# The recurrent layer's gates laid between its projections, a core eviction ahead of a scaling, and the MLP residual by token tile

## What is computed

```
# recurrent layer
u = hn @ w_in + b_in ; x_br = u[:, :1024] ; y_br = gelu(u[:, 1024:])
xc = conv_b + sum over 4 taps of x_br[t-3+tap] * conv_w[tap]
r  = sigmoid(xc_block @ w_ga + b_ga) ; ig = sigmoid(xc_block @ w_gx + b_gx)   # 8 blocks of 128
log_a = -8 * r * softplus(-a_param) ; a = exp(log_a)
b_seq = sqrt(-expm1(2*log_a)) * ig * xc
hs[t] = a[t]*hs[t-1] + b_seq[t]
h = h + (hs * y_br) @ w_o + b_o
# MLP
z = relu(rmsnorm(h) @ w1) ; h = h + (z*z) @ w2
# RWKV-7, after the state scan
y = (y - mean) * rsqrt(var + eps) * lnx_g + lnx_b + bonus * v ; out = (y * silu(g)) @ w_out
```

## Time and profile before

| | us |
|---|---|
| median of 3 runs (lowest to highest) | 1199.31 (1197.18 to 1202.8) |
| the profiled execution | 1200.37 |
| its span | 1198.6 |
| TensorE busy | 1075.3 (90%) |
| GpSimd, ACT, VectorE busy | 706.1, 535.0, 486.0 |
| stretch of the recurrent layer | 332 to 442 |
| second MLP | 443.8 to 623.7 |
| RWKV core and its state steps | 755 to 878 |

### The profile page before, as it was taken

The page is one execution under the profiler, slowest core; times in us unless marked ns, Lnnn a source line. Parts: engine busy times, 40 slices in busy tenths (PEclk is TensorE's granted clock), DMA queues, the critical chain, the costliest instruction groups (busy, mean ns, idle before and its releaser), DMA issues. The chain is left out here.

```text
span 1198.6 us, 19877 instructions
## 1 busy us (share of the span) xinstructions
PE 1075.3 (90%) x8416; PEld 883.7 (74%) x8416; DVE 486.0 (41%) x654; ACT 535.0 (45%) x834; POOL 706.1 (59%) x443
## 2 busy tenths in 40 slices
PE   5999999999977699999988999898898869989685
PEld 4788898998877689999964445798846557767554
DVE  1124274352366725321247266435641451223232
ACT  5537374444436755444421151222223564559352
POOL 6956459988837579989830025300035849667660
PEclk8999999999988899999998999899999979999798
DMA  9642345555634345555572343000036425423140
GB/s 367 235 141 71 133 152 190 191 184 189 193 115 151 123 155 180 192 184 187 191 228 88 114 149 123 20 4 3 4 123 223 159 89 192 133 96 123 62 157 36
DMA packets 45848, 169.37 MB, mean 141 GB/s; under 512 B 5088, under 2 KB 5344, under 8 KB 45440
## 3 DMA queue, kind: packets, MB, share of 16 engines
q1 hardware_dynamic: 43312, 159.06, 39.8%
q0 software_dynamic: 2448, 9.05, 2.4%
HBM read 167.03 MB, written 1.05 MB: 140 GB/s over the span
## 5 line engine op out<-in xcount | busy, mean ns | idle before, releaser
L692 POOL TENSOR_TENSOR ring_r<-ring,high_r 128x512 fp32r<-128x512 f32 (+1 forms) x368 | 635.0, 1755 | 263.5 <-ACT high_r L846 262.2
L846 ACT CAST high_r<-ring 128x1024 fp32r<-128x1024 f32 x248 | 256.5, 1048 | 245.8 <-DMA ring<-w 243.5
L424 PE MATMUL psum<-x_high,high_r 128*128 128x256 f32 x640 | 182.6, 285 | 1.6 <-DVE x_low L282 1.6
L424 PE MATMUL psum<-x_low,high_r 128*128 128x256 f32 x640 | 181.5, 284 | 0.0
L424 PE MATMUL psum<-x_high,ring_r 128*128 128x256 f32 x640 | 181.4, 283 | 0.0
L398 PE MATMUL psum<-high_r,x_high 128*128 128x512 f32 x320 | 131.4, 411 | 13.1 <-DVE x_low L278 9.4
L398 PE MATMUL psum<-ring_r,x_high 128*128 128x512 f32 x320 | 128.7, 402 | 0.0
L398 PE MATMUL psum<-high_r,x_low 128*128 128x512 f32 x320 | 128.7, 402 | 0.0
L600 DVE TENSOR_TENSOR arena<-arena 128x512 f32<-128x512 f32 x32 | 51.7, 1616 | 183.5 <-ACT arena L576 183.4
L424 PEld LDWEIGHTS psum<-x_high,high_r 128*128 128x128 f32 x640 | 123.2, 192 | 2.9 <-issue 1.3
L424 PEld LDWEIGHTS psum<-x_low,high_r 128*128 128x128 f32 x640 | 123.2, 192 | 0.6
(11 more groups left out here) (309 smaller groups left out, 1616.6 us busy)
## 6 DMA issues: line engine op xcount, KB each, us to landing
ring<-w SPq DMA_DIRECT2D x292, 512.0 KB, 3.4
row<-rows POOLq DMA_DIRECT2D x14, 512.0 KB, 8.4
arena<-relt SPq DMA_DIRECT2D x2, 1536.0 KB, 14.8
h<-x SPq DMA_DIRECT2D x1, 1024.0 KB, 5.1
arena<-lora POOLq DMA_DIRECT2D x2, 512.0 KB, 6.2
out<-h SPq DMA_DIRECT2D x1, 1024.0 KB, 4.0
con<-consts SPq DMA_DIRECT2D x1, 529.0 KB, 5.5
arena<-pT POOLq DMA_DIRECT2D x2, 256.0 KB, 4.0
```

The source lines that it names most:

```text
L424: ins = nc.tensor.matmul(out, a, b, start=(k == 0 and q == 0), stop=(k == KT - 1 and q == 2))
L692: ins = nc.gpsimd.tensor_tensor(low(m)[:, part], raw(m)[:, part], read(high(m))[:, part], ALU.subtract)
L846: nc.scalar.copy(high(m), raw(m)).then_inc(high_made, 1)
```

## The change

1. **Residual by tile.** The last row piece of each MLP raises `w2_tile0` when token tile 0 is complete; VectorE adds tile 0 behind that and tile 1 behind the last piece.
2. **Recurrent layer.** The pieces are laid out anew (`REC`, `REC_AT`): x0 to x5, g0, x6, x7, g1, y0, y1, g2, g3, y2 to y7, and TensorE works in that order. ACT evicts x twice (with its bias to `xb`; and with bias `cb` and scale conv_w3, which is the last tap, to `xc`), and VectorE makes the other three taps. The sigmoids become Tanh of half the argument; factors 4 and 0.25 and a "+1" take up the rest. The first half's decays come after gate group 1, the second's after group 3. The products with y, the high copies and the low parts go by quarters instead of halves; the six first casts of W_RO stand ahead of the high copies. GpSimd waits for `scan_done` 2 before W_RO's pieces 0 and 1, and for `og_low` 4 before all later ones. b_o is added after the last low part.
3. **RWKV.** `scale_shift` is cut in `rescale` and `weight_bias`. For the first half they move from ahead of group 1's last eviction to behind `first_state(1)` and behind `next_state(1, 1)`.

```diff
+REC = ["x0", "x1", "x2", "x3", "x4", "x5", "g0", "x6", "x7", "g1", "y0", "y1", "g2", "g3", "y2", "y3", "y4", "y5", "y6", "y7"]
+REC_AT = {name: 4 * W_REC + i for i, name in enumerate(REC)}
...
-            used_piece(dve, w2_piece(m, 7, 3))
             for t in range(NT):
+                if t == 0:
+                    dve.wait_ge(w2_tile0, m + 1)
+                else:
+                    used_piece(dve, w2_piece(m, 7, 3))
...
+                            if c == 7 and f == 3 and t == 0:
+                                ins.then_inc(w2_tile0, 1)
...
+            low_until(4 * W_RO)
+
+            pool.wait_ge(scan_done, 2)
+            low_until(4 * W_RO + 2)
+            pool.wait_ge(og_low, 4)
             low_until(4 * W_RKVG)
...
+            def conv_start(i):
+
+                used_piece(act, REC_AT[f"x{2 * i + 1}"])
                 for j in range(2):
                     f = 2 * i + j
+                    nc.scalar.activation(xb[:, f, 3:], psum[:, i, j * SEQ:(j + 1) * SEQ], ACT.Identity, bias=c8("b_in_x")[:, f:f + 1])
+                    ins = nc.scalar.activation(xc[:, f, :], psum[:, i, j * SEQ:(j + 1) * SEQ], ACT.Identity, bias=cb[:, f:f + 1],
+                                               scale=c8("conv_w3")[:, f:f + 1])
+                ins.then_inc(x_read, 1)
+                split_until(min(REC_AT[f"x{2 * i + 1}"] + 1 + RING, 4 * W_RO))
+
+            def gates_out(i):
+
+                used_piece(act, REC_AT[f"g{i}"])
+                for j in range(2):
+                    f = 2 * i + j
+                    nc.scalar.activation(rg[:, f, :], psum[:, 4 + i % 2, j * SEQ:(j + 1) * SEQ], ACT.Tanh,
+                                         bias=half_ga[:, f:f + 1], scale=0.5)
+                    ins = nc.scalar.activation(ig[:, f, :], psum[:, 6 + i % 2, j * SEQ:(j + 1) * SEQ], ACT.Tanh,
+                                               bias=half_gx[:, f:f + 1], scale=0.5)
                 ins.then_inc(gates_read, 1)
+                split_until(min(REC_AT[f"g{i}"] + 1 + RING, 4 * W_RO))
+
+            split_until(REC_AT["x0"] + RING)
+            conv_start(0)
+            conv_start(1)
+            conv_start(2)
+            act.wait_ge(decay_ready, 1)
+            gates_out(0)
+            conv_start(3)
+            gates_out(1)
...
+            act.wait_ge(gates_read, 2)
+            decays_of(0)
+            gates_out(2)
+            gates_out(3)
             act.wait_ge(gates_read, 4)
+            decays_of(1)
             for q in range(2):
                 act.wait_ge(m2_ready, q + 1)
+                nc.scalar.activation(th[:, 4 * q:4 * q + 4, :], th[:, 4 * q:4 * q + 4, :], ACT.Sqrt,
+                                     scale=0.25).then_inc(m_ready, 1)
             for i in range(4):
+                used_piece(act, REC_AT[f"y{2 * i + 1}"])
...
                 ins.then_inc(y_read, 1)
+                if i >= 1:
+                    split_until(4 * W_RO + 2 * i)
+            for i in range(4):
+                act.wait_ge(o_ready, 5 + i)
+                u = slice(2 * i, 2 * i + 2)
+                nc.scalar.copy(XBH[:, u, :], og[:, u, :]).then_inc(og_high, 1)
...
             nc.vector.memset(xb[:, :, 0:3], 0.0).then_inc(pad_zero, 1)
-            bo = row_of("b_o")
-            dve.wait_ge(xn_ready, 1)
-            for t in range(NT):
-                settle(nc.vector.tensor_tensor(h[:, t, :], h[:, t, :], bo, ALU.add))
             evacuate_low(dve, T_N2, (XH, XL, c8("norm_mix1")))
...
+            og_product(0)
+            for i in range(1, 4):
+                og_product(i)
+                og_low_part(i - 1)
+            og_low_part(3)
+            bo = row_of("b_o")
+            for t in range(NT):
+                settle(nc.vector.tensor_tensor(h[:, t, :], h[:, t, :], bo, ALU.add))
             residual(W_RO)
...
-                        if pp == 1 and b == 1 and s_ == 11:
-                            scale_shift(0)
...
             first_state(1)
-            for g in (1, 2):
-                next_state(1, g)
+            rescale(0)
+            next_state(1, 1)
+            weight_bias(0)
+            next_state(1, 2)
...
+            for i in range(3):
+                rec_in("x", i)
+            rec_gates(0)
+            rec_in("x", 3)
+            rec_gates(1)
+            rec_in("y", 0)
+            rec_gates(2)
+            rec_gates(3)
+            rec_in("y", 1)
+            rec_in("y", 2)
+            rec_in("y", 3)
+            pe_linear(pe, W_RO, 2, xTb2, lambda pe, c: pe.wait_ge(y_read, 2 * c + 2), lambda i: pe.wait_ge(og_low, i + 1))
```

More of the change, by code:

```diff
@@ L21 @@
 RING = 8
-W_QKV, W_O, W_MLP0, W_INX, W_GATES, W_INY, W_RO, W_MLP1 = 0, 6, 8, 24, 26, 27, 29, 31
+W_QKV, W_O, W_MLP0, W_REC, W_RO, W_MLP1 = 0, 6, 8, 24, 29, 31
 W_RKVG, W_OUT_A, W_PLE0, W_KVQG, W_OUT_B, W_PLE1, W_TILES = 47, 55, 57, 60, 68, 70, 73
-PLAIN = {W_GATES, W_PLE0, W_PLE1} | set(range(W_RKVG, W_RKVG + 8))
+REC = ["x0", "x1", "x2", "x3", "x4", "x5", "g0", "x6", "x7", "g1", "y0", "y1", "g2", "g3", "y2", "y3", "y4", "y5", "y6", "y7"]
+REC_AT = {name: 4 * W_REC + i for i, name in enumerate(REC)}
+PLAIN = {W_PLE0, W_PLE1} | set(range(W_RKVG, W_RKVG + 8))
+PLAIN_PIECES = {REC_AT[f"g{i}"] for i in range(4)} | {4 * n + i for n in PLAIN for i in range(4)}
 MLP_TILES = set(range(W_MLP0, W_MLP0 + 16)) | set(range(W_MLP1, W_MLP1 + 16))
@@ L883, in _ @@
             evacuate_high(act, T_N2, (XH, c8("norm_mix1")))
-            split_until(4 * W_INY + 4)
-            for i in range(4):
-                used_piece(act, 4 * W_GATES + i)
+            act.wait_ge(cb_ready, 1)
+            act.wait_ge(pad_zero, 1)
+            def conv_start(i):
+                used_piece(act, REC_AT[f"x{2 * i + 1}"])
                 for j in range(2):
                     f = 2 * i + j
[L889 to L892, removed]
-                ins.then_inc(gates_read, 1)
-                split_until(4 * W_INY + 5 + i)
@@ new lines, in _, with decays_of @@
+            split_until(REC_AT["x0"] + RING)
[6 more added lines that the diff above has]
+            gates_out(1)
+            def decays_of(q):
+                for f in range(4 * q, 4 * q + 4):
+                    nc.scalar.activation(aa[:, f, :], rg[:, f, :], ACT.Exp, bias=nsp8[:, f:f + 1], scale=nsp8[:, f:f + 1])
+                for f in range(4 * q, 4 * q + 4):
+                    ins = nc.scalar.activation(th[:, f, :], rg[:, f, :], ACT.Tanh, bias=sp8[:, f:f + 1], scale=sp8[:, f:f + 1])
+                settle(ins)
+                nc.scalar.activation(bb_[:, 4 * q:4 * q + 4, :], aa[:, 4 * q:4 * q + 4, :], ACT.Square).then_inc(g_ready, 1)
@@ L1264, in _ @@
             nc.vector.memset(xb[:, :, 0:3], 0.0).then_inc(pad_zero, 1)
[L1265 to L1268 removed]
             evacuate_low(dve, T_N2, (XH, XL, c8("norm_mix1")))
[L1270 removed]
             for i in range(4):
[L1272 to L1277, removed]
                 dve.wait_ge(x_read, i + 1)
[L1280 removed]
+                for tap in range(3):
                     wc = c8(f"conv_w{tap}")
@@ L1772, in _, with rec_in, rec_gates @@
             pe.wait_ge(h_ready, 2)
-            for i in range(4):
+            def rec_in(branch, i):
+                if branch == "y":
+                    pe.wait_ge(x_read, i + 1)
                 for j in range(2):
-                    pe_feature_tile(pe, 4 * W_INX + 2 * i + j, psum[:, i, j * SEQ:(j + 1) * SEQ],
-                                    transposed(pe, T_N2) if i == 0 and j == 0 else None)
-            for i in range(4):
+                    pe_feature_tile(pe, REC_AT[f"{branch}{2 * i + j}"], psum[:, i, j * SEQ:(j + 1) * SEQ],
+                                    transposed(pe, T_N2) if branch == "x" and i == 0 and j == 0 else None)
+            def rec_gates(i):
                 pe.wait_ge(xc_ready, i + 1)
@@ L2185, in layout @@
     mlp(0)
-    for c in range(2):
-        feature_tiles(f("rec_w_in")[0], c)
+    rec = {}
+    for b, branch in enumerate("xy"):
+        for c in range(2):
+            feature_tiles(f("rec_w_in")[0], 2 * b + c)
+            rec |= {f"{branch}{4 * c + i}": tiles[-1][:, i * PIECE:(i + 1) * PIECE] for i in range(4)}
+            tiles.pop()
     gates = np.stack([f(n)[0].reshape(4, 2, P, P) for n in ("rec_w_ga", "rec_w_gx")], 1)
-    tiles.append(np.stack([gates, gates], 1).transpose(4, 0, 1, 2, 3, 5).reshape(P, 4096))
-    for c in (2, 3):
-        feature_tiles(f("rec_w_in")[0], c)
+    both = np.stack([gates, gates], 1).transpose(4, 0, 1, 2, 3, 5).reshape(P, 4096)
+    rec |= {f"g{i}": both[:, i * PIECE:(i + 1) * PIECE] for i in range(4)}
+    for n in range(5):
+        tiles.append(np.concatenate([rec[name] for name in REC[4 * n:4 * n + 4]], 1))
     for c in range(2):
```

90 lines of the change are left out of this document (38 added, 52 removed).

## The result

The changed kernel takes 1185.53 us (median of 4 runs, 1184.04 to 1187.61) against 1198.78 for the kernel before on the same chip: ratio 0.9888, 95% interval 0.9869 to 0.9907. That is 13.3 us faster, where 16.7 were forecast. It lies in the range and on the forecast's side. The profiled execution took 1185.72 us, its span is 1183.9.

The account below looks back on a forecast made before the run. The recurrent layer was taken to be bound by the chain behind TensorE (gates, decays, roots, scans, GELU, high copy, low part). 14.0 + 1.4 + 1.3 = 16.7 us gave 1182.6 us; forecast 1180 to 1187, 8-in-10 range 1178 to 1190.

Parts of the forecast that it names:

- Residual by tile: End of both MLPs: adding the first token tile earlier saves 1.4 us at each.
- The chain: Recurrent layer: ACT's queue from y4's arrival to the high copy, without idle time, sets W_RO's start; 14.0 us earlier.
- W_RO's start: Output projection of the recurrent layer: begins at about 402.1 instead of 416.10, the first 1.4 us among the gain.
- decays of a half 4.35: ACT in the recurrent layer: each half's decays take 4.35 us, read from the old trace's two halves.
- y4's load: Recurrent layer: piece y4 arrives 3.7 us after x7 has been used, at 370.1.
- free at the one end, and nearly so at the other: GpSimd's added waits for `scan_done` and `og_low` 4: six low parts end at 420.5 to 422.9, RO7 needed about 424.
- The core's eviction: RWKV core's last eviction ahead of the scaling: gains 1.3 us, not about 4; clock gain between none and 2.4, none taken.
- a gain by the clock as a rival: More full clock at 866 (2.4 us) and at W_RO's start (up to 1): 1179 us; chance 0.11.
- (a): Rival: longer ACT chain from later loads, table loads or scans meeting GpSimd, price 4 to 8 us: 1187 to 1191; chance 0.17.
- (b): Rival: more clock at 866 and W_RO's start, plus a little overlap of the first convolutions: 1179 us; chance 0.11.
- (c): Rival: recurrent reordering does nothing because y's high and low parts wait for each other through the ring: 1195; chance 0.06.
- (d): Rival: GpSimd loses its lead in the second MLP and TensorE stands at each piece: 1207 us; chance 0.04.

Follow-up runs that it names:

- e5: Changed kernel with the decays' Exp and Tanh without their bias operand and gate r made by Square instead of Tanh; ratio 0.9904.
- second profile: Profile of the changed kernel run once more, nothing altered; ratio 0.9904, median 1188.06 against 1199.42 us for the kernel before.
- e7: Changed kernel without GpSimd's wait for the last low part of the gated output (`og_low` 4); ratio 0.9886.
- e11: Changed kernel with the b_o additions back at their old place, ahead of the low parts of x; ratio 0.9884.
- e3: Kernel before with only the last core eviction moved ahead of the scaling; ratio 0.9982.
- e4: Changed kernel with the residual and the core eviction as before, so the recurrent layer's part alone; ratio 0.9914.
- e10: Changed kernel with one more GpSimd wait: no low part of the second MLP before the recurrent layer's residual is in h; ratio 0.9904.
- e6: Changed kernel without GpSimd's wait for the scans (`scan_done` 2); ratio 0.9916.
- e8: Changed kernel with the casts of W_RO's pieces 4 and 5 moved behind ACT's four high copies; ratio 0.9913.
- e9: Changed kernel without GpSimd's `og_low` 4 wait and with casts of W_RO's pieces 4 and 5 behind the second high copy; median 1182.43 us, ratio 0.9869.

## Why the prediction was right or wrong

- **Residual by tile**: right to the tenth at both places (7.2 to 5.9, 9.5 to 8.1).
- **The chain**: right in kind. ACT had no idle time from y4's cast on, the waits before the gate groups were gone, TensorE was ready long before, the scans ran at 2.44, and e5 shows that 1.5 us taken off ACT arrive in full at W_RO. W_RO's start was put at 70.1 us after the MLP's end (402.1 less 332.0) and is at 71.9 and 72.5.
- **The term that was mis-sized**: "decays of a half 4.35". I took the row of the old kernel for an activation that had gained an operand, the bias. It is 5.04 and 5.17; e5 puts the bias at 1.5 us in both halves. The rest of the gap can be read off ACT's rows. In the first profile the decays begin 41.6 us after the MLP's end, where the forecast has 41.5. Half clock had reached into the first x tile, which I had let begin at full clock, and x7 was used at 34.9 instead of 34.4; but y4's load took 3.2 us where I had counted 3.7. Of the 1.8 us that are missing at W_RO, 1.5 lie in the two halves' decays, 0.2 in gates and casts between them and 0.1 in the high copy. The 0.6 us more in the second profile are all ahead of the decays: y4's cast comes 0.3 later (x7 was used at 35.3, after more half clock), and ACT waits 0.3 for y5's weights.
- **GpSimd's wait, "free at the one end, and nearly so at the other"**: wrong by about 1 us. TensorE waits 1.3 us at W_RO's third piece, and W_RO takes 25.3 instead of 24.5; e7 takes the wait away and it takes 23.8. `og_low` 4 came at 405.4, and TensorE was through its first two pieces at 408.7. The forecast worked out only the last piece of the six, at 2.5 to 2.9 us each; at that price the third would have been ready in time, or nearly. It took 4.4 us, because the b_o additions ran beside it. The forecast had asked what GpSimd does to these additions and not what they do to GpSimd; e11, with the wait and without the additions there, has no wait in W_RO.
- **The core's eviction**: right in its main point, that TensorE's end at 862.6 and not the length of the scaling sets the gain (1.3 us); the clock gave 1.1 us more (1.4 in e3), between the bounds of 0 and 2.4 that I had named. Part of that is luck: e4 has 0.8 us of it with the old wait.
- **Clock elsewhere**: the forecast had only a gain by the clock as a rival; the profiled executions lost 2.2 us at an unchanged place.
- By stages, in the first and the second profile: 12.2 and 11.6 up to W_RO, -0.9 in W_RO, 1.4 behind the second MLP, 2.4 and 2.5 at the core. That is 15.1 and 14.6 where the change acts, for 16.7 forecast. The 2.2 and 2.3 lost in the transposes' stretch leave 12.9 and 12.3; the medians say 13.3 and 11.4. The remaining unchanged stages (the start of the program, the core, what follows W_out) differ from the kernel before by -1.4 to 2.6 us, so that the closeness of the sum is in part luck.
- Rivals: (a) in its direction, but mainly by a cause that it didn't name; no table load was added and the scans ran at 2.44, while late arrivals cost 0.3 us in the second profile and up to 1.1 in other runs. Of (b), the clock at the core came, and W_RO began with 3.6 us at half clock instead of 5.1. (c) and (d) are refuted, (d) by e10. Taken one at a time, neither wait given to GpSimd was worth having: one is even (e6), the other costs 1.5 us (e7).

## What to carry to other kernels

When an engine is the chain, price each of its instructions with the operands that it will have, not with the row of its predecessor. Where a slow partner is held back by a semaphore, check the first piece that it then owes, not only the last, and price it beside the work that will run next to it. Before two runs are compared at the end of a chain, look whether the chain began at the same time: in e8 one load that took 1.2 us longer hid a gain of 1.2 us. A step that stands ahead of a critical one costs only what it outlasts the arrival of that one's input: look for who ended the neighbour's idle time (here ACT's, 2.69 us for TensorE) before counting its length.

## What the runs showed of the hardware

An activation of 128x256 with a bias for each partition beside a scale for each partition lets the next one begin after 0.49 us instead of 0.40 with the scale alone (2.07 and 1.70 us for four); with a bias for each partition and a constant scale the gates still took 0.36. A scan of 128x256 takes 0.61 us alone and 1.62 beside GpSimd's subtraction. The same load of a 128x1024 piece took 3.1 to 4.5 us from issue to landing in different runs. And a shorter idle time of TensorE is not by itself a shorter time at half clock: over the ten us after 8.1 us of idling it ran at 0.55 in the changed kernel and at 0.83 in e9, and after 9.5 us in the kernel before at 0.84.
